# Linear attention and merge of a hybrid encoder layer: gate logits first, output transposes in two halves, four gate products ahead of each branch

## The chip, the cores and the metric

The kernel runs on one core of a Trainium2 chip. The metric is the device time of one launch in microseconds (us). All arithmetic is float32 in and out; products that need its precision are made of three passes over a "high" and a "low" part of both operands (the function `three`).

## The reference, cut to what matters

```python
# token mixing, S = D = 1024
proj = rmsnorm(x, g_mix) @ w_in                       # q, k, v, r, gate ranks, latents, gates
o_a  = GLA forward + GLA backward                     # 4 heads, dk 128, dv 256
o_a  = rmsnorm(o_a, gla_onorm) * silu(gr);  y_a = o_a @ w_gla_out
y_b  = MLA(...) @ w_mla_out                           # 8 heads of softmax attention
g    = sigmoid(gates)
x    = x + (g[:, :D] * y_a + g[:, D:] * y_b) @ w_o
# channel mixing: expert choice over 16 SwiGLU experts
x    = x + expert_choice_ffn(x, ...)
```

The log decay of the linear attention (GLA) is `log_sigmoid(rank-16 gate @ w_a2 + b) / 16`, one for each direction.

## The kernel before

The program is written by hand, engine by engine; each engine runs its own list in order, and semaphores tie the lists together. The stages follow one another: the latent projection, eight softmax heads (MLA), four GLA heads, the merge, the output projection, the router and the experts. The change touches the GLA heads and the merge.

**Weights.** Every large weight unit (128 x 1024) goes the same way: SP loads it into `d_raw[n % 2]`, ACT copies it rounded into `d_hi` (`dense_hi(n)`), DVE subtracts (`dense_lo(n)` makes `d_lo`), PE multiplies with both and counts `d_used`. `dense_hi(n)` needs the load and the end of the products of unit n-2. A GLA head has six units (0 and 1 for q and k, 2 to 5 for v and r); from unit 24 on (`MERGE0`) they are the merge's, 16 for each branch.

**A GLA head on PE.** Two rank-16 products give the gate logits of direction 0 in banks 6 and 7 (`gate_logits(h, 0)`, line 848). Then come the products of q and k with unit 1 (`project_qk(h, 1)`, 48 products into banks 0 to 3). Then, for all heads but the first, the 16 transposes of the previous head's output (`outputs_T(h - 1)`, line 698), which take banks 4 to 7, all four. When DVE and ACT have copied these banks out into `oaS` (lines 1379 and 1821, two banks each, counted by `oa_dve` and `oa_act`), the logits of direction 1 go into banks 4 and 5, and the v and r products (`project_vr`, units 2 to 5, eight banks) follow. Later PE makes the scores, the first half of the next head's q and k (`project_qk(h + 1, 0)`), the state updates (line 933, bound to a chain of 14 steps on DVE, line 1475) and the outputs (lines 943 and 945).

DVE turns logits into `zT` (line 1392), ACT makes Abs, Exp and Ln (lines 1845 to 1849), DVE scans (line 1407), ACT makes three Exp tables. In direction 0, DVE makes `d_lo` of unit 2, the two output copies and the logits of direction 1, in this order.

**The merge.** A branch b (0 for GLA, 1 for MLA) has 8 jobs "g" (a gate block, 48 products with `hT`, banks 0/1 or 2/3, then a sigmoid on ACT into `sg`, line 1893) and 8 jobs "y" (a block of the branch's projection, 48 products with `oT_hi` and `oT_lo`, banks 4/5 or 6/7, then a product with `sg` on DVE into `carry`, line 1513). The order is g0 g1 y0 g2 y1 g3 ... y7. The branch input comes back from memory: for b = 0 by two loads into `mT` (the same memory as `carry`), one of six planes and, after the last head's `oaS` is stored (line 539), one of two; for b = 1 plane by plane through the two slots of `stage`. ACT and DVE split it into `oT_hi` (line 1909) and `oT_lo` while PE works on g0 and g1.

All loads and stores named here are issued by SP, in order, on one hardware queue.

Of the kernel before, what the change touches and what calls it, by code (L numbers as in the profile page):

```python
# [55 lines left out]
PAIRS = 2  # L56
# [49 lines left out]
def hybrid_layer(nc, x, positions, g_mix, w_in, gla_wa2_f, gla_ba_f, gla_wa2_b, gla_ba_b, gla_onorm,  # L106
# [25 lines left out]
    with ExitStack() as ctx:  # L132
# [310 lines left out]
        def _(sp):  # L443
# [117 lines left out]
            def load_branch(b):  # L561
                src = (oa_dram, ob_dram)[b]
                if b == 0:
                    sp.wait_ge(oa_out, 16 * (GH - 1))
                    sp.wait_ge(o_ev, GH * NT)
                    sp.dma_start(mT[:, 0:6, :], src[0:6].rearrange("k p s -> p k s")).then_inc(oa_back, 16)
                    store_oa(GH - 1)
                    sp.wait_ge(oa_out, 16 * GH)
                    sp.dma_start(mT[:, 6:8, :], src[6:8].rearrange("k p s -> p k s")).then_inc(oa_back, 16)
                    return  # L570
                for k in range(KD):
                    if k >= 2:
                        sp.wait_ge(oT_lo_ok, KD + k - 1)
                    sp.dma_start(stage[:, k % 2, :], src[k]).then_inc(stage_in[k % 2], 16)

            def load_turn(b, r):
                before = MERGE0 + b * JOBS + r * 4
                for i in range(2):
                    load_job(b, 1, r * 2 + i, 2 + 2 * i, before)
                    load_job(b, 0, r * 2 + i + 2, 3 + 2 * i, before)  # L580

            for b in range(2):
                n = MERGE0 + b * JOBS
                load_job(b, 0, 0, n)
                load_job(b, 0, 1, n + 1)
                if b:
                    sp.wait_ge(ob_out, 32 * MH + CREDIT)
                load_branch(b)
                with sp.Fori(0, 3) as r:
                    load_turn(b, r)  # L590
                load_job(b, 1, 6, n + 14)
                load_job(b, 1, 7, n + 15)
# [34 lines left out]
        def _(pool):  # L627
            for s in (ob_ev, ye_ok, ob_out, ye_free, pv_mm):
                pool.sem_inc(s, CREDIT)
            pool.sem_inc(y_ev, PAIRS)  # L630
# [64 lines left out]
        def _(pe):  # L695
# [156 lines left out]
            def project_qk(h, u, first=False):  # L852

                pe.wait_ge(d_lo_ok, h * GLA_UNITS + u + 1)
                for i in range(4):
                    k = 4 * u + i
                    if first:
                        pe.wait_ge(hT_lo_ok, k + 1)
# [33 lines left out]
            def gla_head(h, first=False, last=False):  # L892
# [33 lines left out]
                if not last:  # L926
                    project_qk(h + 1, 0)
# [1105 lines left out]
```

## Time and profile before

| | |
|---|---|
| median of 3 runs | 2175.2 us (2174.59 to 2183.74) |
| the profiled execution, its own time | 2179.86 us |
| its span | 2178.1 us |
| mean granted TensorE clock | 0.949 |
| PE, DVE, ACT busy | 2006.3, 1300.8, 975.8 us |

PE is busy for 92% of the span; its share is an average over stages with different limits. The granted clock is given as a part of 2.4 GHz: 1.00 is 2.4 GHz, 0.50 is 1.2 GHz. In the timeline an engine's row says when a run of like instructions began, how long it lasted, and in brackets how long the engine had been idle and what released it.

### The profile page before, as it was taken

The numbers are of one execution on the slowest core, as the hardware profiler recorded it, in microseconds if no ns is written. First come the engines' busy times: TensorE is split into PE (matmuls) and PEld (weight loads), VectorE is DVE, ScalarE is ACT, GpSimd is POOL, SyncE is SP. The second block draws the span as 40 slices with busy tenths as digits, with TensorE's granted clock in tenths as the row PEclk, the third lists the DMA queues.
The fourth block names the chain that finished last, engine by engine and source line by source line (L and its number), as shares of the span: only waits on it lengthen the run. The fifth ranks groups of instructions, "written<-read, shape, count | busy, mean of one in ns | idle before, by whom it ended". The sixth has DMA issues, their size and how long they took to land.

```text
span 2178.1 us, 26695 instructions
## 1 busy us (share of the span) xinstructions
PE 2006.3 (92%) x9232; PEld 1645.9 (76%) x9232; DVE 1300.8 (60%) x1664; ACT 975.8 (45%) x1318; POOL 113.4 (5%) x125
## 2 busy tenths in 40 slices
PE   7978899998989999999899989998649999999997
PEld 5577787777767878778688878887647888888886
DVE  3157666677766555464611222344478988989886
ACT  3135444444535233333311121222127787778775
POOL 1000000000000000000000000000000011010100
PEclk9989999999999999999999999999569999999999
DMA  7000000000021110201311231154369999999993
GB/s 243 0 11 21 4 16 20 20 20 20 5 87 54 30 59 20 68 10 58 124 51 48 68 97 48 48 174 193 151 256 339 401 393 400 395 393 402 393 401 93
DMA packets 140418, 306.73 MB, mean 141 GB/s; under 512 B 16208, under 2 KB 70608, under 8 KB 140368
## 3 DMA queue, kind: packets, MB, share of 16 engines
q1 hardware_dynamic: 135760, 289.27, 35.8%
q0 software_dynamic: 4608, 16.78, 3.0%
q8 instruction: 33, 0.54, 0.1%
q14 instruction: 17, 0.14, 0.0%
HBM read 276.64 MB, written 29.36 MB: 140 GB/s over the span
## 4 chain that ended last, share of the span: by engine, by line
PE 75%; DVE 14%; issue 5%; ACT 3%; DMA 1%; POOL 1%; DVEq 0%; ACTq 0%; SPq 0%
PE ps L736 20%; PE ps L738 19%; PE ps L737 19%; PE ps L698 4%; PE ps L759 3%; DVE row_max L1318 3%; PE ps L721 2%; PE ps L722 2%; PE ps L1034 1%; PE ps L933 1%; DVE pT_lo L1124 1%; PE ps L945 1%; ACT pT_hi L1787 1%; PE ps L801 1%; PE ps L800 1%
## 5 line engine op out<-in xcount | busy, mean ns | idle before, releaser
L1124 DVE TENSOR_TENSOR w_lo<-w_raw,w_hi 128x1024 fp32r<-128x1024 f32 x384 | 442.6, 1217 | 57.2 <-ACT w_hi L1953 57.0
L1953 ACT ACTIVATE w_hi<-w_raw 128x1024 fp32r<-128x1024 f32 x384 | 371.0, 1053 | 5.9 <-DMA w_raw<-in_w_gate_e 4.6
L1124 DVE TENSOR_TENSOR d_lo<-d_raw,d_hi 128x1024 fp32r<-128x1024 f32 x72 | 88.1, 1224 | 361.5 <-ACT d_hi L1802 361.3
L1802 ACT ACTIVATE d_hi<-d_raw 128x1024 fp32r<-128x1024 f32 x72 | 76.1, 1058 | 406.7 <-PE ps L738 404.6
L736 PE MATMUL ps<-w_hi,xeT_hi 128*128 128x512 f32 x512 | 202.1, 395 | 4.4 <-DVE w_lo L1124 2.9
L738 PE MATMUL ps<-w_hi,xeT_lo 128*128 128x512 f32 x512 | 200.7, 392 | 0.0
L737 PE MATMUL ps<-w_lo,xeT_hi 128*128 128x512 f32 x512 | 200.7, 392 | 0.0
L736 PE MATMUL ps<-hT_hi,d_hi 128*128 128x512 f32 x384 | 151.1, 394 | 2.6 <-DVE hT_lo L1124 2.6
L736 PE MATMUL ps<-d_hi,hT_hi 128*128 128x512 f32 x384 | 152.7, 398 | 0.5 <-DVE d_lo L1124 0.3
L737 PE MATMUL ps<-d_lo,hT_hi 128*128 128x512 f32 x384 | 151.8, 395 | 0.0
L738 PE MATMUL ps<-d_hi,hT_lo 128*128 128x512 f32 x384 | 151.7, 395 | 0.0
L738 PE MATMUL ps<-hT_hi,d_lo 128*128 128x512 f32 x384 | 150.2, 391 | 0.0
L737 PE MATMUL ps<-hT_lo,d_hi 128*128 128x512 f32 x384 | 150.2, 391 | 0.0
L1772 ACT ACTIVATE probs<-ps,row_max 128x1024 f32<-128x1024 f32 x64 | 71.4, 1116 | 162.1 <-DVE row_max L1318 161.6
L643 POOL TENSOR_TENSOR stat<-stat,minus_half 128x1 f32<-128x1 f32 (+3 forms) x48 | 51.6, 1076 | 1395.3 <-DVE stat L1121 1395.3
L1318 DVE TENSOR_REDUCE row_max<-ps 128x1 f32<-128x1024 f32 x64 | 78.1, 1222 | 66.6 <-PE ps L801 65.8
L1124 DVE TENSOR_TENSOR pT_lo<-ps,pT_hi 128x512 fp32r<-128x512 f32 x128 | 82.4, 686 | 56.5 <-ACT pT_hi L1787 56.3
L736 PEld LDWEIGHTS ps<-w_hi,xeT_hi 128*128 128x128 f32 x512 | 97.1, 190 | 24.7 <-DVE w_lo L1124 3.2
L738 PEld LDWEIGHTS ps<-w_hi,xeT_lo 128*128 128x128 f32 x512 | 97.0, 189 | 20.3
L737 PEld LDWEIGHTS ps<-w_lo,xeT_hi 128*128 128x128 f32 x512 | 97.0, 189 | 19.7
L736 PE MATMUL ps<-oT_hi,d_hi 128*128 128x512 f32 x256 | 100.8, 394 | 5.5 <-DVE d_lo L1124 5.5
L698 PE MATMUL ps<-ident,probs 128*128 128x128 f32 x512 | 73.9, 281 | 32.1 <-DVE pT_lo L1124 32.1
(267 smaller groups left out, 4006.2 us busy)
## 6 DMA issues: line engine op xcount, KB each, us to landing
w_raw<-in_w_gate_e SPq DMA_DIRECT2D x128, 512.0 KB, 7.0
w_raw<-in_w_up_e SPq DMA_DIRECT2D x128, 512.0 KB, 7.1
w_raw<-in_w_down_e SPq DMA_DIRECT2D x128, 512.0 KB, 5.8
d_raw<-in_w_in SPq DMA_DIRECT2D x80, 256.0 KB, 3.0
d_raw<-in_w_o SPq DMA_DIRECT2D x32, 256.0 KB, 3.0
xs<-in_x SPq DMA_DIRECT2D x8, 512.0 KB, 7.1
rows_T<-hT SPq DMA_DIRECT2D x1, 4096.0 KB, 13.0
mla_out_T<-obS SPq DMA_DIRECT2D x16, 256.0 KB, 2.1
```

What stands on the lines that cost most here:

```text
L643: pool.tensor_tensor(dst, dst, minus_half[:, 0:dst.shape[1]], ALU.pow).then_inc(done, 1)
L698: ins = pe.transpose(ps[0:rows, bank, j * P:(j + 1) * P], src, ident[:])
L721: pe.matmul(ps[:, a, 0:LA], lhs, w_lat[:, k, 0:LA], start=k == 0, stop=k == KD - 1)
L736: pe.matmul(out_ap, a_hi, b_hi, start=start, stop=False)
L737: pe.matmul(out_ap, a_hi, b_lo, start=False, stop=False)
L738: return pe.matmul(out_ap, a_lo, b_hi, start=False, stop=stop)
L759: mm = pe.matmul(ps[:, bank, j * width:(j + 1) * width], src[:, k, t * P:(t + 1) * P], w[:, k, :], start=k == 0, stop=k == kc - 1)
L1124: return dve.tensor_tensor(dst, whole, high.bitcast(F32), ALU.subtract)
L1318: dve.tensor_reduce(row_max[:, n:n + 1], ps[:, 2 * (n % 2):2 * (n % 2) + 2, :], mybir.AxisListType.XY, ALU.max, negate=True).then_inc(max_ ...
L1772: nc.scalar.activation(probs[:, n % 3, :].rearrange("p (a c) -> p a c", a=2), ps[:, 2 * (n % 2):2 * (n % 2) + 2, :], ACT.Exp, bias=row_max ...
L1802: nc.scalar.activation(d_hi[:, n % 2, :], d_raw[:, n % 2, :], ACT.Copy).then_inc(d_hi_ok, 1)
L1953: nc.scalar.activation(w_hi[:, n % RING, :], w_raw[:, n % RAW, :], ACT.Copy).then_inc(hi_ok, 1)
```

## The change

It computes the same. In a GLA head both pairs of gate logits are made ahead of the output transposes; these are split into two halves of two banks (6 and 7, used twice), with q and k products between; ACT copies the first half, DVE the second; unit 2 is converted earlier on ACT and DVE. The last head makes half of gate block 0 where the other heads make `project_qk(h + 1, 0)`, and the other half right after its outputs. In the merge four gate blocks lead each branch (`ORDER`), the loops over the blocks are written out, SP loads g2's weights ahead of the store of `oaS`, and ACT waits for that store before its first merge operation. The core of the diff:

```diff
-PAIRS = 2
+
+
+ORDER = ([("g", i) for i in range(4)] + [("y", 0)]
+         + [job for i in range(1, 5) for job in (("y", i), ("g", i + 3))] + [("y", i) for i in range(5, KD)])
+AT = {job: n for n, job in enumerate(ORDER)}
...
+            load_jobs(0, 0, 2)
+            sp.wait_ge(oa_out, 16 * (GH - 1))
+            sp.wait_ge(o_ev, GH * NT)
+            sp.dma_start(mT[:, 0:6, :], oa_dram[0:6].rearrange("k p s -> p k s")).then_inc(oa_back, 16)
+            load_jobs(0, 2, 3)
+            store_oa(GH - 1)
+            sp.wait_ge(oa_out, 16 * GH)
+            sp.dma_start(mT[:, 6:8, :], oa_dram[6:8].rearrange("k p s -> p k s")).then_inc(oa_back, 16)
+            load_jobs(0, 3, JOBS)
+            sp.wait_ge(ob_out, 32 * MH + CREDIT)
+            sp.wait_ge(z_mm, 2 * GH)
+            load_stage(0, 2)
+            load_jobs(1, 0, 6)
+            load_stage(2, KD)
+            load_jobs(1, 6, JOBS)
...
+            def project_vr(h, first):
+
+                pe.wait_ge(d_lo_ok, h * GLA_UNITS + 3)
+                for t in (6, 7, 4, 5, 0, 1, 2, 3):
+                    if t >= 6 and not first:
+                        pe.wait_ge(oa_dve, h * 2 + t - 7)
+                    if t == 4:
+                        pe.wait_ge(z_dve, h * 2 + 2)
+                    if t < 4:
+                        pe.wait_ge(qk_ev, h * 4 + t + 1)
+                    for k in range(2):
+                        mm = vr_product(t, k, 0)
...
+            def outputs_T(h, half, bank=6):
+
+                pe.wait_ge(o_n, h * 2 + half + 1)
+                for j in range(2):
+                    transpose4(bank + j, P, [oR[:, 4 * half + t, j * P:(j + 1) * P] for t in range(4)]).then_inc(o_tr, 1)
 
             def gla_head(h, first=False, last=False):
                 pe.wait_ge(wa_in, h * 64 + 64)
                 if not first:
                     pe.wait_ge(o_ev, h * NT - 2)
                 gate_logits(h, 0)
-                project_qk(h, 1, first)
-                pe.wait_ge(z_dve, h * 2 + 1)
+                project_qk(h, 1, 0, first)
                 if not first:
                     pe.wait_ge(o_ev, h * NT)
-                    outputs_T(h - 1)
-                    pe.wait_ge(oa_dve, h * 2)
+                gate_logits(h, 1)
+                project_qk(h, 1, 1, first)
+                if not first:
+                    pe.wait_ge(z_dve, h * 2 + 1)
+                    outputs_T(h - 1, 0)
+                project_qk(h, 1, 2, first)
+                project_qk(h, 1, 3, first)
+                if not first:
                     pe.wait_ge(oa_act, h * 2)
-                gate_logits(h, 1)
-                for u in range(2, GLA_UNITS):
-                    project_vr(h, u)
+                    outputs_T(h - 1, 1)
+                else:
+                    pe.wait_ge(z_dve, 1)
+                project_vr(h, first)
...
-                if not last:
-                    project_qk(h + 1, 0)
+                if last:
+                    job(0, "g", 0, halves=(0,))
+                else:
+                    for i in range(4):
+                        project_qk(h + 1, 0, i)
...
+            gla_head(GH - 1, last=True)
+            job(0, "g", 0, halves=(1,))
+            pe.wait_ge(o_ev, GH * NT)
+            outputs_T(GH - 1, 0, bank=6)
+            outputs_T(GH - 1, 1, bank=4)
...
+                for kind, i in ORDER[1 - b:]:
+                    if kind == "y" and i == 0:
+                        if b == 0:
+                            pe.wait_ge(oa_dve, 2 * GH)
+                            pe.wait_ge(oa_act, 2 * GH)
+                        pe.wait_ge(oT_lo_ok, KD * b + KD)
+                    job(b, kind, i)
...
+            def second_half_T(h, bank=6):
+                for j in range(2):
+                    dve.wait_ge(o_tr, h * 4 + j + 3)
+                    dve.tensor_scalar(oaS[:, j, HALF:S], ps[:, bank + j, :], onorm_c[:, j:j + 1],
                                       None, ALU.mult).then_inc(oa_dve, 1)
...
                     if d == 0:
                         gate_bias(0)
+                        dense_lo(2, mine)
...
                     if d == 0:
-                        dense_lo(2, mine)
                         if not first:
-                            outputs_even(h - 1)
+                            second_half_T(h - 1)
                         gate_bias(1)
...
+            def branch_lo(b):
...
+            for b in range(2):
+                for n, (kind, i) in enumerate(ORDER):
+                    dense_lo(MERGE0 + b * JOBS + n + 2)
+                    if kind == "g" and i == 1:
+                        branch_lo(b)
+                    if kind == "y":
+                        product(b, i)
+                    if b and kind == "g" and i == KD - 1:
+                        for k in range(5):
+                            merged_lo(k)
+                    if b and kind == "y" and i >= 5:
                         merged_lo(i)
 
...
+            def first_half_T(h):
+                for j in range(2):
+                    act.wait_ge(o_tr, h * 4 + j + 1)
+                    nc.scalar.activation(oaS[:, j, 0:HALF], ps[:, 6 + j, :], ACT.Copy,
                                          scale=onorm_c[:, j:j + 1]).then_inc(oa_act, 1)
...
+                dense_hi(2, mine)
                 for d in range(2):
...
-                    dense_hi((2, 4)[d], mine)
+                    if d == 1:
+                        dense_hi(4, mine)
+                    elif not first:
+                        first_half_T(h - 1)
                     act.wait_ge(b_ok, h * 2 + d + 1)
                     nc.scalar.activation(near[:, d, :], near[:, d, :], ACT.Exp, scale=1 / GATE_DIV).then_inc(e_ok, 1)
                     nc.scalar.activation(qt[:, d, :], bT[:], ACT.Exp, scale=1 / GATE_DIV).then_inc(e_ok, 1)
                     nc.scalar.activation(kt[:, d, :], bT[:], ACT.Exp, scale=-1 / GATE_DIV).then_inc(e_ok, 1)
-                    if d == 0 and not first:
-                        outputs_odd(h - 1)
                     act.wait_ge(tail_ok, h * 2 + d + 1)
                     nc.scalar.activation(kd[:, d, :], zT[:], ACT.Exp, scale=1 / GATE_DIV).then_inc(ed_ok, 1)
                     if d == 0:
+                        take_qk()
                         dense_hi(3, mine)
-                        take_qk()
...
+            first_half_T(GH - 1)
+            act.wait_ge(oa_out, 16 * GH)
+
+
+            def gate(b, i):
+                act.wait_ge(d_used, MERGE0 + b * JOBS + AT["g", i] + 1)
+                if b * KD + i >= 2:
+                    act.wait_ge(y_ev, b * KD + i - 1)
...
+            for b in range(2):
+                for n, (kind, i) in enumerate(ORDER):
+                    dense_hi(MERGE0 + b * JOBS + n + 2)
+                    if kind == "g" and i < 2:
+                        gate(b, i)
+                    if kind == "g" and i == 1:
+                        branch_hi(b)
+                    if kind == "y" and i < 6:
+                        gate(b, i + 2)
+                    if b and kind == "g" and i == KD - 1:
+                        for k in range(5):
+                            merged_hi(k)
+                    if b and kind == "y" and i >= 5:
                         merged_hi(i)
             for g in range(2):
```

The order on PE at the head of a GLA head (`ident,kd` are the transposes of the previous output, `stage,w_a` the gate logits). Before, all transposes stand ahead of the second pair of logits:

```order
L698 MATMUL ps<-ident,kd 128x128 [waits o_n]
L698 MATMUL ps<-ident,kd 128x128 x3
L848 MATMUL ps<-stage,w_a 128x512 [waits oa_act,oa_dve]
L848 MATMUL ps<-stage,w_a 128x512
L869 REGISTER_ALU
L736 MATMUL ps<-d_hi,hT_hi 128x512 [waits d_lo_ok]
```

In the changed kernel, at the same place of a head, first the logits and further down the second half of the transposes:

```order
L735 MATMUL ps<-hT_hi,d_lo 128x512
L845 MATMUL ps<-stage,w_a 128x512 [waits o_ev]
L845 MATMUL ps<-stage,w_a 128x512
L733 MATMUL ps<-hT_hi,d_hi 128x512
...
L895 REGISTER_ALU [waits oa_act]
L695 MATMUL ps<-ident,kd 128x128 [waits o_n]
L695 MATMUL ps<-ident,kd 128x128 x7
L873 REGISTER_ALU
L876 REGISTER_ALU [waits d_lo_ok]
L733 MATMUL ps<-d_hi,hT_hi 128x512 [waits oa_dve]
```

The wait for both copies ahead of the logits is gone; the wait for ACT's copies stands ahead of the second half, and the one for DVE's copies ahead of the first v and r product.

The order on ACT at the start of the merge, before (`oT_hi<-carry` is the branch input, `sg` the gate):

```order
L1821 ACTIVATE oaS<-ps,onorm_c 128x512 [waits o_tr] x2
L1909 ACTIVATE oT_hi<-carry 128x1024 [waits oa_back] x8
L1802 ACTIVATE d_hi<-d_raw 128x1024 [waits d_used,d_in0]
L1893 ACT_TABLE_LOAD
L1893 ACTIVATE sg<-ps 128x1024 [waits d_used]
```

And now:

```order
L1831 ACTIVATE oaS<-ps,onorm_c 128x512 [waits o_tr] x2
L1813 ACTIVATE d_hi<-d_raw 128x1024 [waits d_used,d_in0,oa_out]
L1905 ACT_TABLE_LOAD
L1905 ACTIVATE sg<-ps 128x1024 [waits d_used]
L1813 ACTIVATE d_hi<-d_raw 128x1024 [waits d_used,d_in1]
L1905 ACTIVATE sg<-ps 128x1024 [waits d_used]
L1919 ACTIVATE oT_hi<-carry 128x1024 [waits oa_back] x8
```

The two gates and two weight conversions moved ahead of the branch input, and the first of them waits for `oa_out`, the store of the last head.

The order on SP at the same place, before:

```order
L566 DMA carry<-gla_out_T 128x6x1024 [waits o_ev,oa_out]
L539 DMA gla_out_T<-oaS 128x2x1024 [waits oa_act,oa_dve]
L569 DMA carry<-gla_out_T 128x2x1024 [waits oa_out]
```

And now:

```order
L579 DMA carry<-gla_out_T 128x6x1024 [waits o_ev,oa_out]
L476 DMA d_raw<-in_w_in 128x4x128 [waits d_lo_ok]
L476 DMA d_raw<-in_w_in 128x4x128
L543 DMA gla_out_T<-oaS 128x2x1024 [waits oa_act,oa_dve]
L583 DMA carry<-gla_out_T 128x2x1024 [waits oa_out]
L476 DMA d_raw<-in_w_in 128x4x128 [waits d_lo_ok]
```

The two loads of g2's weights stand ahead of the store.

## Rows read from the trace of the kernel before

**Rows 1.** The waits of PE, 655 to 1075 us: total, times, longest.

```profile
PE ps L848 <- DVE oaS L1379: 10.0, 3, 3.4
```

**Rows 2.** Timeline of GLA head 2: start, us, engine, line, operation, idle before.

```profile
861.44 1.98 PE L848 MATMUL ps<-stage,w_a 16*128 16x512 f32 x4
871.12 1.23 DVE L1400 SCALAR_TENSOR_TENSOR eT<-zT,eT 128x1024 f32<-128x1024 f32 x1 [3.31 <-ACT eT L1849]
874.37 1.91 PE L698 MATMUL ps<-ident,kd 128*128 128x128 f32 x16
876.83 0.17 DVE L1424 TENSOR_TENSOR decay<-qt,near 128x8 f32<-128x8 f32 x1
878.17 1.40 DVE L1379 TENSOR_SCALAR oaS<-ps,onorm_c 128x512 f32<-128x512 f32 x2
879.62 3.78 PE L848 MATMUL ps<-stage,w_a 16*128 16x512 f32 x4 [3.35 <-DVE oaS L1379]
895.94 1.06 ACT L1802 ACTIVATE d_hi<-d_raw 128x1024 fp32r<-128x1024 f32 x1 [7.93 <-PE ps L738]
911.45 1.22 DVE L1439 TENSOR_TENSOR kd<-kd,qk_T 128x1024 f32<-128x1024 f32 x1
928.38 0.81 PE L698 MATMUL ps<-ident,kd 128*128 128x128 f32 x6
```

**Rows 3.** Windows: length, busy and count of each engine, PEclk, DMA share, GB/s.

```profile
879.60:886.40 6.80, 6.78 (x11) 3.64 (x12) 2.96 (x3) 4.73 (x8) 0.00 (x0) 0.50 0.71 231
1065.00:1070.60 5.60, 5.58 (x17) 4.74 (x18) 1.38 (x2) 0.69 (x1) 0.00 (x0) 0.50 0.99 382
```

**Rows 4.** Timeline of ACT, two merge conversions that stand one job apart.

```profile
1112.40 1.06 ACT L1802 ACTIVATE d_hi<-d_raw 128x1024 fp32r<-128x1024 f32 x1 [9.82 <-PE ps L738]
1123.28 1.06 ACT L1802 ACTIVATE d_hi<-d_raw 128x1024 fp32r<-128x1024 f32 x1 [8.90 <-PE ps L738]
```

**Rows 5.** Timeline of GLA head 0: second logits, end of unit 2's products.

```profile
680.02 1.98 PE L848 MATMUL ps<-stage,w_a 16*128 16x512 f32 x4
694.03 1.06 ACT L1802 ACTIVATE d_hi<-d_raw 128x1024 fp32r<-128x1024 f32 x1 [4.09 <-PE ps L738]
```

**Rows 6.** Timeline of the last GLA head: states on PE and on DVE.

```profile
1039.63 3.41 PE L933 MATMUL ps<-vr,qk_T 128*128 128x256 f32 x8 [4.54 <-DVE bT L1461]
1043.47 7.20 DVE L1475 SCALAR_TENSOR_TENSOR carry<-carry,decay,ps 128x256 f32<-128x256 f32 x14
```

**Rows 7.** Timeline of the start of the merge.

```profile
1058.84 1.03 PE L945 MATMUL ps<-carry,qt 128*128 128x256 f32 x4
1061.41 1.09 PE L698 MATMUL ps<-ident,kd 128*128 128x128 f32 x8 [1.55 <-DVE kd L1492]
1065.02 1.97 PE L698 MATMUL ps<-ident,kd 128*128 128x128 f32 x8 [2.52 <-DVE kd L1486]
1067.78 0.39 SPq L539 DMA_DIRECT2D gla_out_T<-oaS  x1
1084.62 1.28 ACT L1893 ACT_TABLE_LOAD   x1
1085.91 1.03 ACT L1893 ACTIVATE sg<-ps 128x1024 f32<-128x1024 f32 x1
1090.70 1.06 ACT L1802 ACTIVATE d_hi<-d_raw 128x1024 fp32r<-128x1024 f32 x1 [3.76 <-PE ps L738]
```

**Rows 8.** DMA issues, KB, us to landing: from 1055 us, then whole span.

```profile
gla_out_T<-oaS SPq DMA_DIRECT2D x1, 1024.0 KB, 8.9
...
gla_out_T<-oaS SPq DMA_DIRECT2D x4, 1024.0 KB, 4.8
```

**Rows 9.** Timeline between the branches.

```profile
1243.02 1.06 ACT L1802 ACTIVATE d_hi<-d_raw 128x1024 fp32r<-128x1024 f32 x1 [9.82 <-PE ps L738]
1266.19 1.22 DVE L1124 TENSOR_TENSOR oT_lo<-stage,oT_hi 128x1024 fp32r<-128x1024 f32 x1 [1.83 <-ACT oT_hi L1909]
1270.13 0.79 PE L736 MATMUL ps<-oT_hi,d_hi 128*128 128x512 f32 x1 [5.45 <-DVE d_lo L1124]
```

More of the change, by code:

```diff
@@ L557, in _, with load_jobs @@
             gla_turn(GH - 1, last=True)
[L561 to L571, printed above, removed]
+            def load_jobs(b, first, last):
+                for n in range(first, last):
+                    kind, i = ORDER[n]
+                    load_job(b, "gy".index(kind), i, MERGE0 + b * JOBS + n)
@@ L572, in load_branch, with load_stage @@
+            def load_stage(first, last):
+                for k in range(first, last):
                     if k >= 2:
                         sp.wait_ge(oT_lo_ok, KD + k - 1)
[L574 to L592, printed above, removed]
+                    sp.dma_start(stage[:, k % 2, :], ob_dram[k]).then_inc(stage_in[k % 2], 16)
@@ L850, in gate_logits @@
                 mm.then_inc(z_mm, 1)
[L852 to L858, printed above, removed]
-                    for j in range(2):
-                        cols = slice((2 * i + j) * P, (2 * i + j + 1) * P)
-                        for half in range(2):
-                            toks = slice(half * HALF, (half + 1) * HALF)
-                            mm = three(ps[:, 2 * j + half, :], d_hi[:, u, cols], d_lo[:, u, cols],
-                                       hT_hi[:, k, toks], hT_lo[:, k, toks], k == 0, k == KD - 1)
-                mm.then_inc(d_used, 1)
@@ L947, in gla_head, with job @@
                     mm.then_inc(o_mm, 1)
-            project_qk(0, 0, first=True)
-            gla_head(0, first=True)
-            with pe.Fori(1, GH - 1) as h:
-                gla_head(h)
-            gla_head(GH - 1, last=True)
-            pe.wait_ge(o_ev, GH * NT)
-            outputs_T(GH - 1)
-            def job(b, kind, i, n, turns=0):
-                k = n % 2
-                pe.wait_ge(d_lo_ok, turns * 4 + n + 1)
-                before = b * KD + i - 1
-                if kind:
-                    pe.wait_ge(y_ev, turns * 2 + before + PAIRS)
-                elif before >= 1:
-                    pe.wait_ge(g_ev, turns * 2 + before)
-                bank = 4 * kind + 2 * (i % 2)
-                rhs_hi, rhs_lo = ((hT_hi, hT_lo), (oT_hi, oT_lo))[kind]
-                for half in range(2):
+            def job(b, kind, i, halves=(0, 1)):
+                n = MERGE0 + b * JOBS + AT[kind, i]
+                k = n % 2
+                pe.wait_ge(d_lo_ok, n + 1)
+                taken = b * KD + i - 1
+                if kind == "g":
+                    if taken >= 1:
+                        pe.wait_ge(g_ev, taken)
+                    bank, rhs_hi, rhs_lo = 2 * (i % 2), hT_hi, hT_lo
+                else:
+                    if taken >= 1:
+                        pe.wait_ge(y_ev, taken)
+                    bank, rhs_hi, rhs_lo = 4 + 2 * (i % 2), oT_hi, oT_lo
+                for half in halves:
                     toks = slice(half * HALF, (half + 1) * HALF)
```

137 lines of the change are left out of this document (43 added, 94 removed).

## The prediction

> **What bounds the kernel now.** I read the table of waits for PE over the heads and the merge, then the timeline around each wait, then windows for the granted clock. PE works without a gap inside a head and inside a branch; two weight conversions that PE releases stand 10.88 us apart [rows 4], which is one job of 48 products, 0.2267 us each. What is left to gain there is the places where PE stands, and what follows them.
>
> The first place is the head of GLA heads 1 to 3. In head 2 PE makes the first logits at 861.44, then 48 products, then 16 transposes from 874.37, and stands 3.35 us before the second logits at 879.62, until DVE and ACT have emptied banks 4 to 7 [rows 2]. It happens 3 times, 10.0 us in all [rows 1]. The clock has fallen meanwhile: from 879.60 to 886.40 the granted clock is 0.50, that is 1.2 GHz, for 6.80 us [rows 3], and work that runs at half speed for 6.80 us costs 3.4 us more than at 2.4 GHz. One such place is therefore worth up to 6.75 us.
>
> The second place is the end of the last head. PE stands 4.54 us ahead of the states at 1039.63 [rows 6], where the other heads have q and k products, then 1.55 and 2.52 us around the last transposes; from 1065.0 the clock is at 1.2 GHz for 5.60 us [rows 3, 7], another 2.8 us. The third is between the branches, 5.45 us [rows 9].
>
> **The change, part by part.** No product, transpose or conversion is added or removed; all terms are waits and clock.
>
> *Heads 1 to 3.* Now two pairs of logits (1.98 us each, the other 0.07 overlapping what follows), 48 products (10.88) and 16 transposes (1.91) run from 861.44 with nothing between that must be waited for: 861.44 + 2 x 1.91 + 10.88 + 1.91 = 878.1. The first half's transposes need `zT` of direction 0, long read by then, and the second half ACT's two copies. These now stand behind Ln, which ended about when DVE's row at 871.12 began; the first half's transposes end about 871.7, so the copies are done by 873, while PE needs them only after 24 more products, at 877.1. The second half is copied by DVE, whose chain is free at 877.0 (876.83 + 0.17), when the first bank is ready at about 877.7. A copy takes 0.7 us (two took 1.40 [rows 2]), so the first v product starts at 878.6, after a wait of 0.5 us; the second bank's copy hides behind 6 products. Unit 2's `d_lo` now lies in the 3.31 us in which DVE waits for Ln [rows 2]; without that cover it would cost its 1.2 us. Unit 2 then ends at 878.6 + 10.9 = 889.5. Before, it ended when ACT was released, at 895.9 [rows 2]: 6.4 us less. I take 6.3 for each of the three heads, **19.0 us**. Bounds: 6.75 at best; at worst a wait of 2.5 us at a handoff brings the low clock back, which leaves 6.3 - 2.0 - 3.4 = 0.9 for each.
>
> The rest of the head must follow. DVE's last product of direction 1 ends at 912.7 and PE's transposes of it begin at 928.4 [rows 2]: 15.7 us of slack against 6.3.
>
> *Head 0.* The second logits leave the place at 680.02; 680.02 + 1.98 + 10.88 = 692.9 against 693.9 [rows 5]: **1.0 us**.
>
> *Last head.* Half of g0 (24 products, 5.4 us) fills the 4.54 us and ends 0.9 us later, at 1040.5. DVE's chain of 14 steps starts at 1043.47 whatever PE does [rows 6], so this delays nothing and the outputs end where they did, at 1059.9 [rows 7]. The other half of g0 runs to 1065.3, the transposes (both normalized by then) to 1067.2, g1 to 1078.1.
>
> Then g2 wants banks 0 and 1, and these wait for ACT's first gate. Behind that gate in ACT's list stand everything else of the merge, the split of the branch input first; ahead of it stand the store of `oaS` (the new wait) and unit 26's conversion. The store is issued at about 1068.4. In the profile it was issued at 1067.78 and landed 8.9 us later, at 1076.7, where the median of four stores is 4.8 [rows 7, 8]: it shares the queue with the load of six planes. Now 0.52 MB of g2's weights goes ahead of it as well. The window from 1065.00 moves 382 GB/s [rows 3], so this adds 1.4 us: 1078.1. Conversion 1.05, table load 1.28, gate 1.03 [rows 4, 7]: g2 starts at 1081.5, after an idle of 3.4 us. An idle of 2.52 and one of 3.35 us were both followed by 1.2 GHz [rows 2, 3, 7], so I charge 2.8 us again. Before, PE was through with g0, g1 and the transposes at 1090.6 [rows 7]; now it is at 1081.5 with 2.8 to come: 1090.6 - 1081.5 - 2.8 = **6.3 us**. The branch input is then split by about 1097, long before y0 at 1106. Bounds: 12.5 if nothing is waited for (1090.6 - 1078.1); 3 if the queue is 3.3 us slower.
>
> The Trainium skill, "DMA: Bandwidth & Descriptors", section on queues, rings and completion order, says that each DMA engine takes the descriptors of one queue in ring order; the 8.9 against 4.8 us agree with it. It speaks against this change, since the new load sits ahead of the store that ACT waits for. The same skill, "ScalarE: Activation LUTs", section on what a table load costs, gives 1.28 us for the load and 1.38 us more for a drain; by it g2 would start 1.4 us later and the sum be 2148.8. The trace shows the gate at 1085.91 right behind the load (1084.62 + 1.28) and no such drain [rows 7].
>
> *Between the branches.* The split of branch 1's input starts when ACT is through with g1 (before: with y7 of branch 0), and in both kernels two jobs cover it. From ACT's release at 1243.02 to the last `oT_lo` at 1267.4 it took 24.4 us, paced by the two slots of `stage`. Then y0's weights still had to be loaded and converted, to 1270.13 [rows 9]; now they are loaded ahead of the planes, and only 1.2 us of `d_lo` follows: 1268.6. **1.5 us**; an idle of 3.9 us and the low clock stay. Bounds: -1, if y1's load, which now also sits ahead of the third plane, pushes the planes back; 4.3, if the idle is short enough to keep the clock (2.8 us more, as above).
>
> *The rest.* Inside a branch y(i+1) and a g run where before one g did; the written-out loops save nothing, since jobs stand 10.88 us apart across the old loop's turns as well [rows 4].
>
> Sum: 19.0 + 1.0 + 6.3 + 1.5 = **27.8 us**. Against the profiled execution, 2179.9 us (span 2178.1 and 1.8 around it), that is 2152.1. That execution lies 4.7 us above the median of the runs, so against the median it is 2175.2 - 27.8 = **2147.4 us**.
>
> **The rivals.**
>
> *No wait at g2* (2141): the store lands soon after its issue, as the other stores do, or the weights pass it. 1068.4 + 4.8 leaves ACT 5 us, and g2 follows g1: 6.2 us more gain. For it: the median of 4.8 [rows 8]. Against: 8.9 at this very place.
>
> *The handoffs through banks 6 and 7 wait* (2163): DVE or ACT comes to its copies late, PE stands 2.5 us and the clock falls in each of three heads; 16 of the 19 us are given back. For it: DVE's chain is free only 0.7 us before it is needed [rows 2].
>
> *It doesn't move the end* (2172): heads lose at the transposes of `kd` what they gained, since DVE's and ACT's chain of direction 1 is what truly paces a head. Against: 15.7 us of slack [rows 2].
>
> *Slower* (2186): inside a branch a g job takes the banks of a gate that is made only after a y product. After y ends come conversion 1.06, `d_lo` 1.2, product 1.2, sum 1.2 and gate 1.0, 5.7 us, and one job of 10.88 covers it [rows 4]. It decides from a chain of about 13 us on: 2.1 us of wait and 2.8 of clock at each of g4 to g7 in two branches is 39 us, against 27.8. Nothing in the rows comes near it.
>
> **How the numbers follow.** Forecast 0.62 (own range 2141 to 2154), no wait at g2 0.17, handoffs 0.11, no effect 0.07, slower 0.03. A measurement of this kernel can tell about 0.5%, 11 us, from no change. Faster: 0.62 + 0.17 + 0.08 of the handoffs = 0.87; same 0.03 + 0.07 = 0.10; slower 0.03. The range reaches from no wait at g2 with the best of the other bounds (2138) to the handoffs (2163).
>
> **What the profile will show.** PE's second logits a fourth of the way into the q and k products, without idle and at clock 1.00 at the head of every GLA head, and unit 2's products of head 2 through 28 us after the first logits instead of 34.4; half of g0 ahead of the last states; an idle of about 3.4 us at g2 that ends on ACT's gate, with the store's landing behind it; about 4 us at branch 1's y0. Wrong would be: waits at the first v product above 1 us, a fallen clock in the heads, or no idle at g2.

## The result, and the profile after

The changed kernel runs in 2149.45 us (median of 4 runs, 2143.16 to 2150.83) against 2175.43 us (4 runs, 2174.59 to 2183.74) for the kernel before, measured beside it: ratio 0.9866, 95% interval 0.9835 to 0.9898. That is 26.0 us less, where 27.8 us were forecast. The profiled execution took 2150.83 us, its span 29.0 us shorter than that of the kernel before.

To see where the time went, I cut both spans at four rows of DVE: the logits of head 0, the first masking of the last head's second half of scores, and the last product of each branch. Timeline of DVE, the kernel before (start, duration, line, operation):

```profile
669.19 1.28 DVE L1392 TENSOR_SCALAR zT<-ps,b_a 128x1024 f32<-128x1024 f32 x1 [5.07 <-PE ps L848]
1032.64 0.68 DVE L1455 TENSOR_TENSOR zT<-ps,keep_hi 128x512 f32<-128x512 f32 x1
...
1245.25 1.22 DVE L1513 TENSOR_TENSOR carry<-ps,sg 128x1024 f32<-128x1024 f32 x1
...
1427.61 1.22 DVE L1515 TENSOR_TENSOR sg<-ps,sg 128x1024 f32<-128x1024 f32 x1
```

The same rows of the changed kernel:

```profile
671.08 1.28 DVE L1406 TENSOR_SCALAR zT<-ps,b_a 128x1024 f32<-128x1024 f32 x1 [5.08 <-PE ps L845]
1014.11 0.68 DVE L1469 TENSOR_TENSOR zT<-ps,keep_hi 128x512 f32<-128x512 f32 x1
...
1218.68 1.22 DVE L1527 TENSOR_TENSOR carry<-ps,sg 128x1024 f32<-128x1024 f32 x1
...
1398.63 1.22 DVE L1529 TENSOR_TENSOR sg<-ps,sg 128x1024 f32<-128x1024 f32 x1
```

The heads take 343.03 us instead of 363.45, **20.4 less**. From there to the last product of branch 0 it is 204.57 instead of 212.61, **8.0 less**, and from there to the last product of branch 1 179.95 instead of 182.36, **2.4 less**. These are all the stages the change touches, 30.9 us together. The rest of the span is the same to 0.02 us (750.49 and 750.47), and the stages ahead of the heads, in which nothing was changed, took 1.9 us more in this execution.

*Heads, for [rows 1, 2].* Timeline of head 2 of the changed kernel:

```profile
855.67 1.98 PE L845 MATMUL ps<-stage,w_a 16*128 16x512 f32 x4
860.53 1.98 PE L845 MATMUL ps<-stage,w_a 16*128 16x512 f32 x4
865.30 1.03 PE L695 MATMUL ps<-ident,kd 128*128 128x128 f32 x8
871.63 1.03 PE L695 MATMUL ps<-ident,kd 128*128 128x128 f32 x8
872.27 1.41 DVE L1393 TENSOR_SCALAR oaS<-ps,onorm_c 128x512 f32<-128x512 f32 x2 [1.04 <-PE ps L695]
873.08 0.50 PE L733 MATMUL ps<-d_hi,hT_hi 128*128 128x512 f32 x1 [0.41 <-DVE oaS L1393]
884.29 1.06 ACT L1813 ACTIVATE d_hi<-d_raw 128x1024 fp32r<-128x1024 f32 x1 [5.34 <-PE ps L735]
```

The idle of 3.35 us is gone; at the first v product PE still waits 0.41 us for DVE's copy. Unit 2's products are through 28.6 us after the first logits, against 34.5 before. The window over the whole place has the clock at 1.00, where it was 0.50 for 6.80 us [rows 3] (columns: length, busy and count of each engine, clock, DMA share, GB/s):

```profile
855.60:884.00 28.40, 27.99 (x121) 21.00 (x121) 22.25 (x28) 15.32 (x22) 1.01 (x1) 1.00 0.23 74
```

*Start of the merge, for [rows 6, 7].* Timeline:

```profile
1021.84 1.89 PE L949 MATMUL ps<-vr,qk_T 128*128 128x256 f32 x8
...
1024.93 7.20 DVE L1489 SCALAR_TENSOR_TENSOR carry<-carry,decay,ps 128x256 f32<-128x256 f32 x14
...
1046.65 1.91 PE L695 MATMUL ps<-ident,kd 128*128 128x128 f32 x16
...
1049.60 0.39 SPq L543 DMA_DIRECT2D gla_out_T<-oaS  x1
...
1058.62 1.06 ACT L1813 ACTIVATE d_hi<-d_raw 128x1024 fp32r<-128x1024 f32 x1 [10.07 <-DMA gla_out_T<-oaS]
1059.70 1.28 ACT L1905 ACT_TABLE_LOAD   x1
1060.99 1.02 ACT L1905 ACTIVATE sg<-ps 128x1024 f32<-128x1024 f32 x1
1062.16 0.60 PE L733 MATMUL ps<-hT_hi,d_hi 128*128 128x512 f32 x1 [2.71 <-ACT sg L1905]
```

The last states now follow g0's half without idle (4.54 us before), and DVE's chain of states starts 18.54 us sooner, just as the scores do. The 16 transposes run in one piece. Then PE waits 2.71 us at g2 for ACT's gate, and what the gate waits for is the store: issued at 1049.60, landed at 1058.62. Over the next 3.84 us the granted clock averages 0.56. *Between the branches, for [rows 9],* the idle is 4.15 us instead of 5.45, and a low clock follows again (0.55 over 3.48 us):

```profile
1264.02 0.76 PE L733 MATMUL ps<-oT_hi,d_hi 128*128 128x512 f32 x1 [4.15 <-issue]
```

Windows of the changed kernel behind the two idles, for [rows 3]:

```profile
1062.16:1066.00 3.84, 3.84 (x10) 3.02 (x11) 0.00 (x0) 0.84 (x1) 0.00 (x0) 0.56 1.09 347
...
1264.02:1267.50 3.48, 3.48 (x9) 2.75 (x10) 1.03 (x1) 0.00 (x0) 0.00 (x0) 0.55 0.68 169
```

### The profile page after: what moved, and what is told of

It is laid out like the page before. It is cut to its first block, busy times and chain, and to the rows that moved or that the text cites. A ratio compares the mean times of both kernels' runs of the same rounds, so it can differ in the third digit from the quotient of the medians.

```text
span 2149.1 us, 26412 instructions
## 1 busy us (share of the span) xinstructions
PE 1993.5 (93%) x9232; PEld 1639.2 (76%) x9232; DVE 1300.1 (60%) x1664; ACT 976.8 (45%) x1318; POOL 113.3 (5%) x125
## 4 chain that ended last, share of the span: by engine, by line
PE 78%; DVE 12%; issue 5%; ACT 3%; DMA 2%; POOL 0%; SPq 0%; DVEq 0%; ACTq 0%
PE ps L733 20%; PE ps L734 20%; PE ps L735 20%; PE ps L695 4%; PE ps L756 3%; DVE row_max L1333 3%; PE ps L718 2%; PE ps L719 2%; PE ps L961 1%; PE ps L1049 1%; PE ps L949 1%; DVE pT_lo L1139 1%; ACT pT_hi L1798 1%; PE ps L798 1%; PE ps L797 1%
```

## The experiments

Nine other kernels and the changed kernel once more were run, each beside the kernel before. Times of whole runs spread by up to 0.6% in one kernel (2170.64 to 2184.03 for that of before), which is more than some of the terms. So each run is read by its profile as well, cut at the rows above; each profile is one execution. Stages in us ("ahead of the heads" ends at the first of these rows):

| run | ratio to before (95%) | ahead of the heads | heads | to end of branch 0 | branch 1 |
|---|---|---|---|---|---|
| before | 1 | 669.19 | 363.45 | 212.61 | 182.36 |
| the change | 0.9866 (0.9835 to 0.9898) | 671.08 | 343.03 | 204.57 | 179.95 |
| heads alone | 0.9928 (0.9909 to 0.9946) | 665.11 | 343.02 | 213.08 | 182.21 |
| merge alone | 0.9951 (0.9934 to 0.9968) | 665.48 | 360.93 | 203.48 | 180.07 |
| no half g0 | 0.9897 (0.9879 to 0.9915) | 661.78 | 343.07 | 213.41 | 180.74 |
| store first | 0.9829 (0.9808 to 0.9850) | 671.13 | 343.03 | 200.01 | 177.55 |
| split early | 0.9824 (0.9804 to 0.9845) | 662.66 | 343.02 | 204.57 | 174.08 |
| both of these | 0.9807 (0.9787 to 0.9828) | 668.36 | 343.02 | 199.99 | 174.08 |
| second logits late | 0.9846 (0.9827 to 0.9865) | 666.59 | 340.92 | 202.85 | 180.16 |
| g2 weights behind store | 0.9856 (0.9834 to 0.9878) | 664.71 | 343.04 | 202.09 | 180.04 |
| all three | 0.9791 (0.9768 to 0.9814) | 668.43 | 340.94 | 199.97 | 174.08 |
| the change again | 0.9844 (0.9821 to 0.9867) | 668.76 | 343.13 | 204.29 | 179.82 |

What is left of the span is 750.1 to 753.1 us in all of them.

**1. The heads alone.** The kernel before with the edits of the heads as in the diff; the merge stays as it was, but the last head's output transposes use the new halves:

```diff
+            outputs_T(GH - 1, 0, bank=6)
+            outputs_T(GH - 1, 1, bank=4)
...
+            first_half_T(GH - 1)
+            act.wait_ge(oa_dve, 2 * GH)
```

> The kernel before with the change's GLA heads alone (both logits lead, transposes two banks at a time through banks 6 and 7, normalization by halves); last head's end, merge and branches as before. My theory (the terms add): heads 1 to 3 give 6.4 us each and head 0 one, 20.4 us in all, so 2175.2 - 20.4 = 2154.8 us, ratio 0.9906; the first v product of heads 1 to 3 waits 0.5 us and the clock stays at full speed there; 4.5 us of idle ahead of the last head's states are still there, and so are 1.55 and 2.52 us at the last transposes. Rival 1 (handoffs): what the heads gain shows only together with the merge: 2171, PE waits of 2 us and a clock of 0.5 in each head. Rival 2 (the whole gain is from the heads): 2149.4, the same as with the whole change.

The median is 2161.6 us, 15.7 us less by the ratio (12 to 20), 5 us short of what I expected. The stage of the heads itself is exactly that of the change, 343.02 us, 20.4 us less; the first v products wait 0.4 to 0.5 us, the idles of 4.5, 1.5 and 2.5 us at the last head are there. The profiled execution spans 2156.5 us, 21.6 less than that of before, though its part ahead of the heads was 4.1 shorter and the rest behind the branches 2.6 longer. By the stages both rivals are wrong: the heads gain without the merge, and the merge's stages stay as they were.

**2. The merge alone.** The changed kernel with `project_qk`, `project_vr`, `outputs_T` and the copies of `oaS` as before:

```diff
-                gate_logits(h, 1)
-                project_qk(h, 1, 1, first)
...
+                    outputs_T(h - 1)
+                    pe.wait_ge(oa_dve, h * 2)
+                    pe.wait_ge(oa_act, h * 2)
+                gate_logits(h, 1)
```

> The changed kernel with the heads of before (all 16 transposes between the two logits, four banks), keeping half of g0 inside the last head, four g products leading each branch, and the new order of loads. My theory: start of the merge 8.0 us and between the branches 2.4 us, 10.4 in all: 2164.8 us, ratio 0.9952; g2 waits 2.7 us for ACT's first gate and y0 of branch 1 waits 4.2 us. Rival (the gain is from the heads, the merge only moves its waits): 2175, the same as before. If the terms add, this run's gain and that of the heads alone make the whole 26 to 31 us.

By the ratio it is 10.7 us less, by stages 9.1 and 2.3. With run 1 the whole runs make 26.4 us, against 26.0 for the change: the terms add. The stages of the two runs make 34.1, 3.2 more than the 30.9 of the change, and the clock roughly accounts for it. In the heads of this run the old idles of 3.25, 3.35 and 3.34 us are back, but in the 6.8 us behind the first of them the clock is 0.75 and behind the others 0.50; this head alone is 2.7 us shorter than in the kernel before, the next 1.2 longer, and the stage of the heads 2.5 shorter. And behind the idle at g2, here 3.19 us, no low clock followed, which cost the change 1.7 us.

**3. No half of g0 in the last head.**

```diff
-                if last:
-                    job(0, "g", 0, halves=(0,))
-                else:
+                if not last:
...
-            job(0, "g", 0, halves=(1,))
             pe.wait_ge(o_ev, GH * NT)
             outputs_T(GH - 1, 0, bank=6)
             outputs_T(GH - 1, 1, bank=4)
+            job(0, "g", 0)
```

> The changed kernel with g0 of branch 0 made whole behind the last transposes; the four g products still lead both branches. My theory: the half g0 is what pays at the start of the merge and the lead of four there gives nothing of its own. PE stands 4.5 us ahead of the last states, 1.5 and 2.5 us at the transposes, then works through g0 to g3 without the wait of 2.7 us at g2, and all of the 8.0 us are lost: 2149.4 + 8 = 2157.4 us, y7 of branch 0 8.0 us later against the last head's chain of states than with the change. Rival (the lead of four g pays at branch 0 by itself): at most 3 us lost, 2152.

The stage of branch 0 is 213.41 us, 8.8 more than with the change and no better than before. So this term needs the half g0, which fills an idle of 4.54 us. The lead of four g gives branch 0 nothing of its own: g2's wait does not occur, but it did not exist before either. Whether the half g0 would give as much without that lead, with y0 right behind g1, no run shows. Between the branches the idle was 3.57 us.

**4. The store ahead of the six planes.**

```diff
-            load_jobs(0, 0, 2)
+            load_jobs(0, 0, 3)
+            store_oa(GH - 1)
             sp.wait_ge(oa_out, 16 * (GH - 1))
             sp.wait_ge(o_ev, GH * NT)
             sp.dma_start(mT[:, 0:6, :], ...)
-            load_jobs(0, 2, 3)
-            store_oa(GH - 1)
```

> The changed kernel with the last head's store of oaS issued ahead of the load of the six planes of oa (3.1 MB), behind g2's weights. My theory (the store lands late because 3.1 MB of planes and 0.5 MB of weights stand ahead of it on its queue): it lands about 5 us after its issue instead of 9.0, ahead of the end of g1, the wait of 2.7 us at g2 goes and the low clock of 3.8 us with it (1.9 us): 4.6 us less than the change, 2144.8 us; the six planes land at most 9 us after the store and their split starts when ACT is through with the second gate, as before. Rival 1 (landing takes 9 us whatever stands ahead): no change, 2149.4. Rival 2 (the six planes now come too late and y0 waits): g3 to y0 leave 30 us for it, so it should not show; it would be 2152 or more.

The stage is 4.56 us shorter, as worked out. DMA rows of the store (KB, us from issue to landing), the changed kernel:

```profile
gla_out_T<-oaS SPq DMA_DIRECT2D x1, 1024.0 KB, 9.0
```

And this run, with its timeline at the first gate:

```profile
gla_out_T<-oaS SPq DMA_DIRECT2D x1, 1024.0 KB, 5.1
```

```profile
1054.75 1.06 ACT L1812 ACTIVATE d_hi<-d_raw 128x1024 fp32r<-128x1024 f32 x1 [6.13 <-DMA gla_out_T<-oaS]
...
1057.13 1.03 ACT L1904 ACTIVATE sg<-ps 128x1024 f32<-128x1024 f32 x1
```

The gate is made while g1 still runs and PE does not wait. Branch 1 was 2.4 us shorter as well, though nothing was changed there: the idle at its y0 was 3.18 us instead of 4.15, and this time no low clock followed. Why it was shorter is not shown. In the other kernels with the change's branch 1 (the change, runs 2, 3, 7, 8 and 10) it was 3.57 to 4.30 us.

**5. Three planes of branch 1 split early.**

```diff
-            load_jobs(1, 0, 6)
-            load_stage(2, KD)
+            load_jobs(1, 0, 5)
+            load_stage(2, 5)
+            load_jobs(1, 5, 6)
+            load_stage(5, KD)
...
+                    if b and n == 0:
+                        branch_hi(b, 0, 3)
                     if kind == "g" and i == 1:
-                        branch_hi(b)
+                        branch_hi(b, 3 * b)
```

(`branch_lo` on DVE likewise; the two arguments are the first plane and the one behind the last.)

> The changed kernel with the first three planes of branch 1's input split right behind the gate of g0 of branch 1 (ACT and DVE), the other five behind the gate of g1 as now; planes three to five are loaded ahead of y1's weights. My theory (the idle at branch 1's y0 is the tail of a split of eight planes that starts after g1 and needs 25.8 us from ACT's release, where g2 and g3 cover 21.8): three planes earlier are about 8 us, so the split ends some 4 us ahead of the end of g3, the idle of 4.15 us is gone and the low clock of the 4 us behind it (1.5 us) too: 5.6 us less than the change, 2143.8 us; last product of branch 0 to last product of branch 1 174.4 us instead of 179.95. Rival 1 (the pace is the planes' loads beside the weights, whatever ACT does): the idle stays above 3 us, 2149. Rival 2 (gate 1 now comes late and g3 waits for its banks): an idle at g3, 2150 or more.

The stage is 5.87 us shorter. The last rows of the split:

```profile
1243.86 1.06 ACT L1923 ACTIVATE oT_hi<-stage 128x1024 fp32r<-128x1024 f32 x1 [2.93 <-DMA stage<-mla_out_T]
1244.82 1.04 ACT L1817 ACTIVATE d_hi<-d_raw 128x1024 fp32r<-128x1024 f32 x1
1244.95 1.23 DVE L1141 TENSOR_TENSOR oT_lo<-stage,oT_hi 128x1024 fp32r<-128x1024 f32 x1 [2.77 <-ACT oT_hi L1923]
1251.54 1.06 ACT L1817 ACTIVATE d_hi<-d_raw 128x1024 fp32r<-128x1024 f32 x1 [5.67 <-PE ps L737]
```

The split ends at 1246.2 and PE is through with g3 at 1251.5: 5.3 us of slack where PE had stood 4.15. The planes still wait for loads, so the pace is as before; only the start moved. g3 does not wait for its banks.

**6. Both.**

> Both edits: the last head's store ahead of the six planes, and three planes of branch 1 split early. The run with the store first took 12.6 us off the time from the last head's states' scores to the last product of branch 0 against the kernel before, 4.56 more than the change did. If both terms add: 4.6 + 5.6 = 10.2 us less than the change, 2139.2 us, ratio to the kernel before 0.9820 by the profile's stages, with no idle of PE over 2 us from the first head to the end of branch 1. Rival (one hides the other): 2144.

The stages are 199.99 and 174.08 us, 10.45 less than with the change: each edit gives in its own stage what it gave alone. The 2.4 us that branch 1 was shorter in run 4 do not come on top, since the early split has already closed that idle. The ratio, 0.9807 (0.9787 to 0.9828), is lower than that of either edit alone, but the intervals overlap; that the edits add is read from the stages.

**7. The second logits late.**

```diff
                     pe.wait_ge(o_ev, h * NT)
-                gate_logits(h, 1)
+                else:
+                    gate_logits(h, 1)
...
                     outputs_T(h - 1, 1)
+                    gate_logits(h, 1)
                 else:
```

> The changed kernel with the second pair of logits of heads 1 to 3 put back behind all q and k products and both pairs of transposes; transposes still go two banks at a time through banks 6 and 7. It tells the two halves of the heads' edit apart. My theory (what paid is that nobody empties four banks ahead of the second logits; where the logits stand is nearly free): PE makes the second logits without a wait, the first v products take banks 6 and 7 behind them, and v product 4 waits at most 0.5 us for DVE's read of the logits; time from first logits to first logits of the next head 94.4 us, as with the change; 2149.4 us, within 2. Rival (the lead of the second logits itself is what pays, since DVE's and ACT's chain of direction 1 starts 14 us later and the transposes of kd wait for it): 5 us or more of wait in each of three heads at the transposes of kd or at v product 4, 2165 or more.

By its stage it is better than the change: the heads take 340.92 us, 2.1 less; by whole runs the two can't be told apart (0.9846 against 0.9866 and 0.9844). Timeline of its head 2:

```profile
864.29 1.03 PE L695 MATMUL ps<-ident,kd 128*128 128x128 f32 x8
865.25 1.98 PE L845 MATMUL ps<-stage,w_a 16*128 16x512 f32 x4
...
866.18 1.41 DVE L1395 TENSOR_SCALAR oaS<-ps,onorm_c 128x512 f32<-128x512 f32 x2 [0.15 <-DVE decay L1441]
...
878.42 1.06 ACT L1815 ACTIVATE d_hi<-d_raw 128x1024 fp32r<-128x1024 f32 x1 [4.68 <-PE ps L735]
```

The logits stand directly behind the transposes and hide DVE's copies, so the wait of 0.41 us at the first v product is gone too. The lead of the second logits, half of the edit's text, was not what paid: without it heads 1 to 3 are no slower. The 0.41 us are a part of the 0.7 us that each head gains; the rest I can't assign. The stage to the end of branch 0 is 1.7 us shorter too, in code that this edit does not touch: the low clock behind g2 did not follow here.

What paid in the heads is, then, in what is left of the edit, and two things in it were never taken apart: that the transposes need only banks 6 and 7, so that nobody must empty four banks before PE goes on, and that ACT and DVE convert unit 2 earlier and ACT's copies moved up its list. The row of the kernel before that bears on it is DVE's conversion of unit 2, which stood right ahead of its two copies:

```profile
877.03 1.22 DVE L1124 TENSOR_TENSOR d_lo<-d_raw,d_hi 128x1024 fp32r<-128x1024 f32 x1
```

An estimate from it and [rows 2]: with that conversion moved and all four banks kept, DVE's copies would have ended at 877.0 + 1.4 = 878.4 instead of 879.6, and 1.2 of the 3.35 us would have gone. So the two halves are the likelier cause of most of the idle's end, but how much each part gives, the clock included, is not shown.

**8. g2's weights behind the store.**

```diff
-            load_jobs(0, 2, 3)
             store_oa(GH - 1)
+            load_jobs(0, 2, 3)
```

> The changed kernel with g2's weights (0.52 MB) issued behind the last head's store, the six planes still ahead of it. It measures the term of 1.4 us that the prediction charged for these weights ahead of the store. By that term the store lands 1.4 us sooner after its issue (7.6 instead of 9.0 us) and the wait at g2 falls from 2.7 to 1.3 us; 2148.0 us. Rival (the weights share the queue with the planes but the 3.1 MB of planes alone set the landing, which the store of the kernel before took 8.9 us for, or ACT then waits for the weights instead): landing 8.9 to 9.0 us or a wait of the conversion for the weights, no change, 2149.4.

Both theories hold in part. The store lands 6.6 us after its issue, 2.4 sooner than in the changed kernel with the weights ahead (I had charged 1.4); its DMA row and ACT's next row in the timeline:

```profile
gla_out_T<-oaS SPq DMA_DIRECT2D x1, 1024.0 KB, 6.6
```

```profile
1051.36 1.06 ACT L1813 ACTIVATE d_hi<-d_raw 128x1024 fp32r<-128x1024 f32 x1 [9.18 <-issue]
```

It landed at 1049.8, but ACT's conversion, the next in its list, started at 1051.36: it now waits for the weights. PE's wait fell from 2.71 only to 1.82 us. The stage is 2.5 us shorter, 0.9 of it wait and 1.6 clock, which stayed at 1.00 behind this idle.

The landing itself differs from one execution to the next. With weights and planes ahead it took 8.7 to 9.7 us (the change and runs 2, 3, 5, 7 and 10). With the planes alone ahead it took 6.6 us here, 7.1 in run 1 and 8.9 in the kernel before, though in run 1 the store is issued behind the planes at the same distance, 6.4 us. With the planes behind it, it took 5.1 us (run 4). The order on the queue matters, but the 2.4 us for the weights and the 1.5 for the planes (6.6 against 5.1) are each a difference of single readings.

**9 and 10. All three edits that paid, and the change again.**

> The changed kernel with all three edits that paid by their stages: the last head's store ahead of the six planes (4.56 us), three planes of branch 1 split early (5.87 us), and the second logits of heads 1 to 3 behind the last transposes (2.1 us). If they add by stages against the change: 12.5 us less, so heads 340.9, last head's scores to the last product of branch 0 200.0, last product of branch 0 to that of branch 1 174.1 us; about 2149.4 - 12.5 = 2136.9 us, ratio to the kernel before 0.981 or a little lower. Rival (the clock or another wait takes some back): 2142.

> The changed kernel itself again, beside the run with all three edits and the kernel before, to see the ratio on one chip and how far the stages that the change does not touch move from one execution to the next (671.1, 665.1, 661.8, 662.7 us up to the first head's logits so far, in kernels with the same code there). Expected: ratio to the kernel before 0.987 within 0.003; heads 343.0, then 204.6 and 180.0 us as in its first profile; the stages ahead of the heads anywhere from 661 to 671 us.

All three edits run in 2132.0 us (2131.47 to 2136.55), 0.9791 of the kernel before (0.9768 to 0.9814), against 0.9844 (0.9821 to 0.9867) for the change beside it; the two intervals don't overlap. Its stages are those of the runs 6 and 7. In the table of PE's waits between 655 and 1425 us one row is left over 1 us:

```profile
PE ps L952 <- DVE carry L1492: 1.7, 1, 1.7
```

The changed kernel, run again, had the same stages within 0.3 us, while the part ahead of the heads took 668.8 us instead of 671.1.

## Why the prediction was right, and where it was off

**Heads: right, with two errors that cancel.** 20.0 us were charged for the four heads, 20.4 measured; the wait at the first v product was forecast as 0.5 us and is 0.41 to 0.50, and the clock stays up. But head 2, from which the 6.3 us for each head were worked out, gained 5.9 us (28.6 us to the end of unit 2's products, where 28 were forecast), and head 1 gained 6.8 (101.1 us from its first logits to those of head 2 before, 94.3 now), which is over the bound of 6.75. Behind the idles of heads 1 and 3 the low clock had lasted longer than in head 2. Windows of 2.3 us that begin 6.8 us behind these two idles, in the kernel before (PE alone; clock third from the end):

```profile
785.20:787.50 2.30, 2.30 (x7) 0.52 0.72 208
986.60:988.90 2.30, 2.30 (x7) 0.52 0.74 219
```

In head 2 the clock is back at 1.00 there. One head stood for three, and it was the one with the shortest low clock.

The 15.7 us of slack held, since the whole gain passed on to the end of the last head. The handoffs in banks 6 and 7 cost no more than the 0.5 us, and "it doesn't move the end" fell with the run of the heads alone. (Its 2172 us does not follow from the sum either: without the 20.0 us of the heads that gives 2167.4.) What I did not see is which part of the edit earns this: run 7 earns more with the logits at the old place.

**Start of the merge: right mechanism, sizes off.** The term was 6.3 us, measured 8.0. The idle at g2 was forecast as 3.4 us and is 2.71, since the store landed 9.0 us after its issue, not 9.7. For the low clock 2.8 us were charged; 3.84 us at 0.56 lose 1.7. Together that is 1.8 us, against a difference of 1.7. The 2.8 had been taken from a place where an idle of 1.55 us stands shortly before the one of 2.52 [rows 7]. That the landing came out near the forecast is luck: the weights ahead cost 2.4 us in run 8, not 1.4, and the 8.9 us of before [rows 8], the base for the rest, was a high reading, 7.1 us in run 1 in the same order. "No wait at g2" was wrong for the change and right for run 4, which shows that the queue's order was the reason. "DMA: Bandwidth & Descriptors" of the Trainium skill, section on queues, rings and completion order, was cited against the change; runs 4 and 8 agree with it, 5.1, 6.6 and 9.0 us as less or more stands ahead. By another page of the Trainium skill, "ScalarE: Activation LUTs", section on what a table load costs, g2 would have waited (an estimate from the page's figure) 1.4 us longer; the gate again starts 1.29 us after the start of the table load (1060.99 and 1059.70), right behind it, so the trace does not agree.

**Between the branches: small and low.** Charged 1.5, measured 2.4: the idle fell by 1.3 as forecast. The rest, 1.1 us, is clock. Windows behind the idle of the kernel before (all engines, clock third from the end):

```profile
1270.13:1274.13 4.00, 4.00 (x9) 3.13 (x10) 1.23 (x1) 1.39 (x2) 0.00 (x0) 0.50 0.61 166
1274.13:1276.13 2.00, 2.00 (x7) 1.60 (x6) 0.00 (x0) 0.00 (x0) 0.00 (x0) 0.66 0.66 192
```

These windows lose 2.0 and 0.7 us; now 3.48 us at 0.55 lose 1.6. I had assumed that the low clock would stay as it was.

**The rival "slower":** no g4 to g7 waited; products stand 10.88 us apart inside both branches.

**The sum.** 27.8 us were forecast for the touched stages; they are 30.9 us shorter in the profile, and the medians differ by 26.0, with an interval from 22 to 36. That the total came within 2 us of the forecast is in part luck: the three terms were each too small, and what lies outside the touched stages took the surplus back. Of these 4.9 us, 1.9 are seen in the profiles, as the longer part ahead of the heads. The other 3.0 are that the profiled execution of before lies 4.4 us above the median of its runs and that of the changed kernel only 1.4; where the other executions differ is not shown, since they have no profile. The likeliest place is the part ahead of the heads, which took 661.8 to 671.1 us in kernels with the same code there. The window over most of it has a clock of 0.95 in the changed kernel,

```profile
160.00:650.00 490.00, 443.93 (x2268) 371.23 (x2268) 339.67 (x504) 234.87 (x394) 22.90 (x14) 0.95 0.07 24
```

and of 0.98 in the run without half of g0 in the last head:

```profile
160.00:650.00 490.00, 435.55 (x2265) 360.75 (x2263) 341.69 (x504) 237.61 (x397) 25.62 (x19) 0.98 0.08 26
```

A difference of this size can decide which of two medians 5 us apart looks better. The 15.7 us of run 1, where its stages give 20.1, may be such a case, but this is not shown either.

## What to carry to other kernels

Look for what must be emptied before the bound engine may go on, and try to shrink that (here two banks twice instead of four at once, with the conversion moved out of the way) before reordering the engine's work: of the two parts of the edit in the heads, the reordering turned out to be worth nothing. An engine's wait that stands at the head of its list, here for a store, makes everything queued ahead of that transfer part of the bound engine's path: put the small transfer that is waited for ahead of the big one that isn't. And where a chain of conversions is too long for its cover, start a part of it one job earlier.

For measuring: where executions differ by 0.3% in stages that weren't touched, cut the profile at the same rows in every run. The changed kernel's stages then repeated within 0.3 us from one profile to the other. But look at the clock and at the idles in the stage before giving a term of 2 us to an edit: untouched stages moved by 1.7 us (run 7) and 2.4 us (run 4).

## What the runs showed of the hardware that I had not expected

I took it that an idle of 2.5 us or more is followed by 1.2 GHz. The rows behind the waits at g2 and at branch 1's y0 show that between 2.4 and 3.2 us it went either way. Windows of 4 us behind the idle (length, PE busy and count, clock, DMA share, GB/s), the change again after 2.43 us:

```profile
1059.67:1063.67 4.00, 4.00 (x11) 0.57 1.07 340
```

Second logits late, after 2.60 us at g2:

```profile
1055.44:1059.44 4.00, 4.00 (x18) 1.00 1.06 336
```

Merge alone, after 3.19 us at g2 and 4.30 us at y0:

```profile
1074.95:1078.95 4.00, 4.00 (x18) 1.00 1.08 347
1275.38:1279.38 4.00, 4.00 (x12) 0.63 0.76 200
```

Of the idles at g2, 2.43, 2.71 and 2.73 us were followed by the low clock, 1.82, 2.60 and 3.19 us were not; at y0 3.18 us was not, and all from 3.57 to 5.45 us were. So the same wait may cost 1.7 us more or nothing, from kernel to kernel of nearly the same code. Closing such a wait wholly, as runs 4 and 5 do, takes the chance out of it.
